# Running the joins between stages of a two-block transformer kernel in two halves of the tokens

## The chip, the cores and the metric

The kernel runs on one core of one Trainium2 chip. The metric is the device time of one execution in microseconds (us), over three runs. A profile is one further execution, recorded instruction by instruction. The engines are PE (matrix multiply; PEld is its weight load), DVE (elementwise), ACT (elementwise with functions), POOL (small elementwise work and some loads) and SP (which issues the weight loads).

## The reference, cut to what matters

256 tokens of width 1024, all in fp32. After a first block (mLSTM, attention and a mixture of experts) and a norm, two layers follow:

```
for l in range(2):
    x = x + 0.5 * rmsnorm(swiglu(rmsnorm(x, ffn1_pre_g[l]), w_ffn1_in[l], w_ffn1_out[l]), ffn1_post_g[l])
    h = rmsnorm(x, mix_pre_g[l])
    z, xbc, dt, rq, rk, rv, rg, aq, ak, av, gate = split(h @ w_in[l])
    ...                      # three mixers and their gated sum y
    x = x + rmsnorm(y @ w_out[l], mix_post_g[l])
    x = x + 0.5 * rmsnorm(swiglu(rmsnorm(x, ffn2_pre_g[l]), w_ffn2_in[l], w_ffn2_out[l]), ffn2_post_g[l])
```

Each `x = x + rmsnorm(...)` followed by the next `rmsnorm(x, ...)` is a join: the residual of a token needs that token's whole output row, and the next stage's first product needs the normalised row, transposed.

## The kernel before

A layer has three stages, called f1 (the first feed-forward), mx (the mixers) and f2. PE accumulates into 8 banks of 128 x 512 fp32. `LAYER_JOBS` lists all uses of the banks in order, and each engine waits on a bank's "full" or "read" counter. Weights come in units of 128 x 2048 (1 MB) through a ring of 6 slots; SP loads unit i into slot i % 6 once the unit 6 places before it is given back (`load_units`). A layer has 121 units, so its last unit sits in slot 0, the slot that the next layer's first unit wants; at the start of a layer SP waits for `ring_free`, raised by ACT at the end of f2.

Most products are done in three fp32r passes ("hi" and "lo" parts of both operands). `unit_hi` (ACT) rounds a unit to its hi part in one of 3 buffers, `unit_lo` (DVE) makes the lo part in `ring_r`. PE waits for the lo part (`unit_parts`). A feed-forward unit of the input projection takes 48 matmuls (2 halves of the bank, 8 slices of the depth, 3 passes) of 128x128 weights on 256 moving columns, the tokens (`split_columns`). The output projection keeps four banks, (n, t) for column half n and token half t, and goes through 11 units; each unit takes 24 matmuls on 512 moving columns, the tokens being the weights. mx begins with row products (rq first), also with tokens as weights and 512 moving columns: 12 matmuls for each unit and token half.

A join before the change runs in this order, all of it for the 256 tokens together:

- ACT squares the four output banks (`post_scalar`), DVE scales them into `xn` (`post_vector`), POOL makes the root (`post_pool`), DVE updates x for t = 0 and t = 1.
- ACT squares x for t = 0 and t = 1 (`row_squares`), after hi part 0 of the next stage, and then makes hi part 1; DVE has lo part 0 in its queue ahead of `scale_rows`; POOL makes the second root (`pre_pool`).
- DVE scales x into `xn`, t = 0 and 1; PE transposes 16 blocks into 4 banks (`turn_rows`); ACT writes the hi columns, DVE the lo columns, bank by bank; the first matmuls of the next stage wait for them bank by bank.

There are six such joins: from the experts into f1 of layer 0 (the chain there has one norm more, L2332, since the first block ends in its own norm), f1 to mx and mx to f2 in each layer, and f2 of layer 0 to f1 of layer 1, where the loop over the layers turns. After the last f2 only the update of x and the store of the output follow.

Of the kernel before, what the change touches and what calls it, by code (L numbers as in the profile page):

```python
# [8 lines left out]
P = 128  # L9
# [41 lines left out]
HI_BUFFERS = AHEAD_UNITS + 1  # L51

# [99 lines left out]

class Banks:
# [39 lines left out]
class Units:  # L193
# [4 lines left out]
    def __init__(self, landed_sems, parts_sem, units, base, parts_base, B, l=None):  # L198
        self.landed_sems, self.parts_sem, self.base, self.B, self.l = landed_sems, parts_sem, base, B, l
        self.parts_base = parts_base  # L200
# [3 lines left out]
        self.per = [len(range(s, len(units), SLOTS)) for s in range(SLOTS)]  # L204
        parts = [n for n in self.names if self.ends[n] is None]
        self.part = {n: i for i, n in enumerate(parts)}

    def slot(self, name):
        return self.index[name] % SLOTS

    def landed(self, name):

        i = self.index[name]
        n = self.base[i % SLOTS] + i // SLOTS + 1
        n = n if self.l is None else self.l * self.per[i % SLOTS] + n
        return self.landed_sems[self.slot(name)], n * 16

    def given_back(self, name):
# [4 lines left out]
        return self.parts_sem, (n if self.l is None else self.l * len(self.part) + n)  # L223

# [803 lines left out]
def moe_scalar(act, m, ps, M):  # L1028
    raise_ahead(act, M, "scalar")
    turns = act.value_load(m.r.turns_i[0:1, 1:2], min_val=PAIRS, max_val=PAIRS * PASSES)  # L1030
    with act.Fori(0, turns) as i:
# [24 lines left out]
def moe_tensor(pe, m, ps, M, landed):  # L1056
# [11 lines left out]
    with pe.Fori(0, turns) as i:  # L1068
# [13 lines left out]
        pe.wait_ge(M["added"], since(i * 4))  # L1082
# [73 lines left out]
def unit_hi(act, m, U, F, names, j, his):  # L1156

    if j >= HI_BUFFERS:
        act.wait_ge(*U.given_back(names[j - HI_BUFFERS]))
    act.wait_ge(*U.landed(names[j]))  # L1160
    act.activation(his[j % HI_BUFFERS], m.ring[U.slot(names[j])], ACT.Copy).then_inc(F["unit_hi"], 1)  # L1161


def unit_lo(dve, m, U, F, f, names, j, his):
# [3 lines left out]
    dve.tensor_tensor(m.ring_r[slot], m.ring[slot], his[j % HI_BUFFERS].bitcast(F32), ALU.subtract).then_inc(  # L1168
# [3 lines left out]
def unit_parts(pe, m, U, F, f, names, j, his, k):  # L1172

    pe.wait_ge(*F.at("unit_lo", SPLIT_BEFORE[f] + j + 1))
    return [v.rearrange("p (k n) -> p k n", k=k) for v in (his[j % HI_BUFFERS], m.ring_r[U.slot(names[j])])]


def split_columns(pe, B, ps, job, parts, moving, cols=None):


    hi, lo = parts
    for c in range(2):
        for k in range(KT):
# [12 lines left out]

def ffn_tensor(pe, m, ps, B, U, F, f):

    names = [f"{f}.n.{i}" for i in range(4)]
    units = ffn_unit_names(f)  # L1200
    turn_rows(pe, B, names, ps, m.xn, m.c["ident"], F, f)

    for i in range(FT):
# [3 lines left out]
        split_columns(pe, B, ps, job, parts, (m.hT_r, m.hTlo_r), [B.drained(n) for n in names] if i == 0 else None)  # L1207
    for i in range(FT // 2):
        hi, lo = unit_parts(pe, m, U, F, f, units, FT + i, m.whi_r, 2)
        for k in range(2):  # L1210
            kk = 2 * i + k
            pe.wait_ge(*F.at("ffn_hid", sofar(f, FT) + kk + 1))
            for n in range(2):
                for t in range(TT):
                    job = f"{f}.out.{n}.{t}"
                    if kk == 0:
                        B.claim(pe, job)
                    turns = passes_of([x[:, kk, t * P:(t + 1) * P] for x in (m.hid_r, m.hidlo_r)],
                                      [w[:, k, n * 512:(n + 1) * 512] for w in (hi, lo)])
                    for q, (x, w) in enumerate(turns):  # L1220
                        mm = pe.matmul(ps[B.bank(job)][:], x, w, start=kk + q == 0, stop=kk == FT - 1 and q == 2)  # L1221
                    if kk == FT - 1:
                        mm.then_inc(B.full(job), 1)
        if i < FT // 2 - 1:
            mm.then_inc(U.parts_sem, 1)


def ffn_scalar(act, step, m, ps, B, U, F, f, gain):
    units = ffn_unit_names(f)
    unit_hi(act, m, U, F, units, 0, m.whi_r)  # L1230
    row_squares(act, m, F, f)
    for j in range(1, AHEAD_UNITS):
        unit_hi(act, m, U, F, units, j, m.whi_r)
    for i in range(4):
        job = f"{f}.n.{i}"
        act.wait_ge(*B.filled(job))
        for k in range(2):
            ins = act.activation(m.hT_r[:, 2 * i + k, :], ps[B.bank(job)][:, k * T:(k + 1) * T], ACT.Copy,
                                 scale=gain[:, 2 * i + k:2 * i + k + 1])
        ins.then_inc(F[f"{f}.cols"], 1)  # L1240
# [13 lines left out]
    post_scalar(act, m, ps, B, F, f)  # L1254


def row_squares(act, m, F, f):

    for t in range(TT):
        act.wait_ge(*F.at(BEFORE[f] + ".x", t + 1 if f != "f1" else t - 1))  # L1260
        act.activation(m.hrows[:, t, :], m.x[:, t, :], ACT.Square, scale=D ** -0.5,
                       accum_out=m.ss[:, t:t + 1]).then_inc(F[f"{f}.ss"], 1)


def post_scalar(act, m, ps, B, F, f):

    for n in range(2):
        for t in range(TT):
            job = f"{f}.out.{n}.{t}"
            act.wait_ge(*B.filled(job))  # L1270
            act.activation(m.hrows[:, t, n * 512:(n + 1) * 512], ps[B.bank(job)][:], ACT.Square, scale=D ** -0.5,
                           accum_out=m.halves[:, n, t:t + 1]).then_inc(F[f"{f}.pss"], 1)
    if f == "f2":
        act.sem_inc(F["ring_free"], 1)


def ffn_vector(dve, step, m, ps, B, U, F, f, gain, post, post_landed=None):
    units = ffn_unit_names(f)
    unit_lo(dve, m, U, F, f, units, 0, m.whi_r)
    scale_rows(dve, m, F, f)  # L1280
    for i in range(4):
        job = f"{f}.n.{i}"
        dve.wait_ge(*F.at(f"{f}.cols", i + 1))
        for k in range(2):
            kk = 2 * i + k
            ins = dve.scalar_tensor_tensor(out=m.hTlo_r[:, kk, :], in0=ps[B.bank(job)][:, k * T:(k + 1) * T],  # L1286
# [1229 lines left out]
```

## Time and profile before

| what | value |
|---|---|
| median of three runs | 2398.27 us (2396.99 to 2401.87) |
| span of the profiled execution | 2400.0 us |
| busy: PE, DVE, ACT | 92%, 50%, 46% |
| POOL busy | 1% |
| mean DMA rate | 203 GB/s |

The profiled execution's own time is its span, 2400.0 us from first to last instruction, which is 1.7 us above the median and inside the range of the runs. A high busy share says that PE is the engine to look at, not that all of its time is needed.

### The profile page before, as it was taken

How to read it: one execution, taken by the hardware profiler on the slowest of the kernel's cores; microseconds unless marked ns; L12 is line 12 of the kernel's file. 1: busy time of each engine (PE TensorE's matmuls, PEld its weight loads, DVE VectorE, ACT ScalarE, POOL GpSimd, SP SyncE). 2: the span in 40 equal slices, each digit the busy share in tenths (PEclk: the TensorE clock that was granted, in tenths of full speed). 3: DMA queues.
4: the chain of work that ended last, by engine and by line, in shares of the span. 5: the costliest groups of instructions: out<-in, count | busy, mean ns of one | idle time of the engine just before them, and what ended most of it. 6: DMA issues, size and time to landing. Idle time of an engine off the chain costs nothing.

```text
span 2400.0 us, 33677 instructions
## 1 busy us (share of the span) xinstructions
PE 2212.8 (92%) x13178; PEld 1771.5 (74%) x13178; DVE 1198.0 (50%) x1568; ACT 1099.0 (46%) x1365; POOL 35.5 (1%) x59
## 2 busy tenths in 40 slices
PE   7857999999997998999999899979989999998998
PEld 6734444433445996898889799879968988897996
DVE  1152333333335664664745566456654655446663
ACT  1310000000004993454445599479734634364992
POOL 0000000000000000000000000000000000000000
PEclk9977999999999999999999999989989999998999
DMA  6205999999994554442235455355545422354552
GB/s 245 88 0 213 421 410 401 401 401 400 401 386 160 183 184 168 171 163 101 75 122 178 158 196 177 123 208 188 185 148 191 145 86 88 125 190 162 177 187 94
DMA packets 66920, 486.09 MB, mean 203 GB/s; under 512 B 7424, under 2 KB 7424, under 8 KB 8544
## 3 DMA queue, kind: packets, MB, share of 16 engines
q1 hardware_dynamic: 65632, 476.07, 52.8%
q0 software_dynamic: 1152, 8.16, 0.9%
q8 instruction: 91, 1.49, 0.2%
q14 instruction: 45, 0.37, 0.1%
HBM read 483.15 MB, written 1.05 MB: 202 GB/s over the span
## 4 chain that ended last, share of the span: by engine, by line
issue 68%; PE 26%; DVE 2%; ACT 2%; POOL 1%; DMA 0%; ACTq 0%; DVEq 0%; POOLq 0%; SPq 0%
PE bank L1077 9%; PE bank L1102 5%; PE bank L362 4%; PE bank L1051 3%; PE bank L1112 3%; PE bank L377 1%; PE bank L753 1%; PE bank L326 0%; ACT work L1042 0%; ACT work L1039 0%; DMA work<-in_first 0%; PE bank L1091 0%; ACT work L435 0%; POOL sums L308 0%; POOL sums L309 0%
## 5 line engine op out<-in xcount | busy, mean ns | idle before, releaser
L1188 PE MATMUL bank<-work_parts 128*128 128x256 f32 x2368 | 618.1, 283 | 0.0
L1168 DVE TENSOR_TENSOR ring_parts<-ring,work_parts 128x2048 fp32r<-128x2048 f32 x208 | 475.5, 2291 | 218.3 <-ACT work_parts L1161 197.6
L1161 ACT ACTIVATE work_parts<-ring 128x2048 fp32r<-128x2048 f32 x208 | 396.3, 1908 | 199.4 <-PE bank L1221 98.2
L1188 PEld LDWEIGHTS bank<-work_parts 128*128 128x128 f32 x2368 | 437.0, 192 | 0.1
L1188 PE MATMUL bank<-columns_parts,work_parts 128*128 128x256 f32 x1408 | 400.3, 284 | 2.3 <-DVE work_parts L1286 2.3
L1188 PE MATMUL bank<-columns_parts,ring_parts 128*128 128x256 f32 x1408 | 399.1, 283 | 0.0
L1188 PEld LDWEIGHTS bank<-columns_parts,work_parts 128*128 128x128 f32 x1408 | 271.0, 192 | 3.9 <-DVE work_parts L1286 3.8
L1188 PEld LDWEIGHTS bank<-columns_parts,ring_parts 128*128 128x128 f32 x1408 | 271.0, 192 | 0.0
L362 PE MATMUL bank<-columns,ring 128*128 128x256 f32 x1152 | 254.5, 383 | 1.2 <-ACT columns L344 1.2
L362 PEld LDWEIGHTS bank<-columns,ring 128*128 128x128 f32 x1152 | 220.7, 192 | 34.1 <-issue 3.7
L1221 PE MATMUL bank<-work_parts 128*128 128x512 f32 x704 | 217.4, 389 | 0.0
L1077 PE MATMUL bank<-ring,work 128*64 128x512 f32 x768 | 168.3, 594 | 1.1 <-DVE work L1024 1.1
L1221 PEld LDWEIGHTS bank<-work_parts 128*128 128x128 f32 x704 | 132.2, 188 | 27.4
L1077 PEld LDWEIGHTS bank<-ring,work 128*64 128x64 f32 x768 | 54.4, 137 | 112.5 <-issue 112.5
L1221 PE MATMUL bank<-ring_parts,work_parts 128*128 128x512 f32 x352 | 137.0, 389 | 0.0
L1019 DVE TENSOR_TENSOR x<-x,bank 128x512 f32<-128x512 f32 x64 | 44.0, 688 | 171.8 <-PE bank L1112 171.8
L1188 PE MATMUL bank<-rows_parts,work_parts 128*128 128x256 f32 x448 | 127.0, 283 | 0.0
L1188 PE MATMUL bank<-rows_parts,ring_parts 128*128 128x256 f32 x448 | 126.8, 283 | 0.0
L1102 PE MATMUL bank<-work 128*64 128x512 f32 x512 | 113.6, 594 | 14.1 <-ACT work L1039 14.1
L1382 PE MATMUL bank<-work_parts 128*128 128x512 f32 x320 | 115.7, 393 | 0.0
L1296 DVE TENSOR_TENSOR work<-work,bank 128x256 f32<-128x256 f32 x88 | 37.1, 422 | 155.2 <-ACT work L1251 155.2
L1250 ACT ACT_TABLE_LOAD x88 | 112.9, 1283 | 1.6
(355 smaller groups left out, 2917.9 us busy)
## 6 DMA issues: line engine op xcount, KB each, us to landing
ring<-in_w_layers SPq DMA_DIRECT2D x242, 1024.0 KB, 4.8
ring<-in_w_experts SPq DMA_DIRECT2D x96, 1024.0 KB, 8.0
work<-in_w_experts SPq DMA_DIRECT2D x96, 1024.0 KB, 9.1
ring<-in_w_first SPq DMA_DIRECT2D x16, 1024.0 KB, 4.9
work<-in_post POOLq DMA_DIRECT2D x3, 1024.0 KB, 5.0
work<-in_second POOLq DMA_DIRECT2D x1, 2944.0 KB, 14.3
work<-in_first SPq DMA_DIRECT2D x1, 1641.5 KB, 8.9
x<-in_x SPq DMA_DIRECT2D x1, 1024.0 KB, 5.0
```

Of the source, the lines that this page charges most:

```text
L362: mm = pe.matmul(ps[B.bank(job)][:, c * T:(c + 1) * T], w[:, k, c * P:(c + 1) * P], moving[:, k, :], start=k == 0, stop=k == KT - 1)
L1019: dve.tensor_tensor(xs, xs, ps[(SUM, TURN)[q % 2]][:], ALU.add).then_inc(M["added"], 1)
L1051: mm = pe.matmul(ps[GATHER + g][:, k * P:(k + 1) * P], m.xn[:, t, kk * P:(kk + 1) * P], m.sel[:, t, :], start=t == 0, stop=t == TT - 1)
L1077: mm = pe.matmul(ps[bank][e * 64:e * 64 + 64, :], m.hc[:, h * 4 + k, e * 64:e * 64 + 64], both[e][:, k, :], start=h + k == 0, stop=h * 4 + ...
L1102: mm = pe.matmul(ps[DOWN + n][e * 64:e * 64 + 64, :], m.hidT[:, ff * P + e * 64:ff * P + e * 64 + 64], both[e][:, f, n * 512:(n + 1) * 512 ...
L1112: pe.matmul(ps[(SUM, TURN)[q % 2]][:], m.selgT[:, t * P:(t + 1) * P], m.ym[:, n * 512:(n + 1) * 512], start=True, stop=True).then_inc(M["s ...
L1161: act.activation(his[j % HI_BUFFERS], m.ring[U.slot(names[j])], ACT.Copy).then_inc(F["unit_hi"], 1)
L1168: dve.tensor_tensor(m.ring_r[slot], m.ring[slot], his[j % HI_BUFFERS].bitcast(F32), ALU.subtract).then_inc(F["unit_lo"], 1)
L1188: mm = pe.matmul(ps[B.bank(job)][:, c * T:(c + 1) * T], w, x, start=k + n == 0, stop=k == KT - 1 and n == 2)
L1221: mm = pe.matmul(ps[B.bank(job)][:], x, w, start=kk + q == 0, stop=kk == FT - 1 and q == 2)
L1250: step(act.activation(e, e, ACT.Ln, bias=1.0))
L1382: mm = pe.matmul(ps[B.bank(jobs[t])][:], x, w, start=kk + n == 0, stop=kk == KT - 1 and n == 2)
```

## The change

At each join the tokens go in two halves of 128.

- The last products of a stage are reordered so that the banks of t = 0 are full first: in f1 and f2 the last two output units (`HELD_UNITS`) are held and used for t = 0, then t = 1 (12 matmuls a bank); in mx the last pair of units is used by half. A fourth hi buffer makes room for this.
- `bridge_scalar`, `bridge_vector` and `bridge_pool` replace the post and pre functions: roots of one column, x, its squares and `xn` for each half, t = 0 while PE still works on t = 1.
- In joins inside a layer hi and lo parts 0 and 1 of the next stage are made ahead of the bridge (`next_unit`), and the columns of half 0 inside it (`next_columns`). In f1, after the experts or the turn of the loop, they are made behind the bridge: two hi parts, then the columns.
- The next stage's first work goes by half: in f1 and f2 units 0 and 1 are multiplied on 128 tokens at a time (`split_half`, same weights loaded again for the other half); in mx, rq goes by half, still on 512 moving columns.
- `LAYER_SLOTS` puts two neighbouring units into slot 0, so that the next layer's first units find slots given back earlier. `ring_free` goes.

```diff
-def split_columns(pe, B, ps, job, parts, moving, cols=None):
...
+def split_half(pe, B, ps, job, parts, moving, t, ready=None):
+    bank = ps[B.bank(job)]
+    tokens = slice(t * P, (t + 1) * P)
     for c in range(2):
         for k in range(KT):
+            if ready and c == 0 and k % 2 == 0:
+                pe.wait_ge(*ready[k // 2])
+            for n, (w, x) in enumerate(passes_of([w[:, k, c * P:(c + 1) * P] for w in parts],
+                                                 [x[:, k, tokens] for x in moving])):
+                mm = pe.matmul(bank[:, c * T + t * P:c * T + (t + 1) * P], w, x, ...)
...
 def ffn_tensor(pe, m, ps, B, U, F, f):
-    turn_rows(pe, B, names, ps, m.xn, m.c["ident"], F, f)
-    for i in range(FT):
+    turn_half(pe, B, ps, m, F, f, 0)
+    split_half(pe, B, ps, f"{f}.in.0", parts0, moving, 0, [F.at("half_lo", ...) for i in range(4)])
+    turn_half(pe, B, ps, m, F, f, 1)
+    split_half(pe, B, ps, f"{f}.in.1", parts1, moving, 0)
+    split_half(pe, B, ps, f"{f}.in.0", parts0, moving, 1, [B.drained(f"{f}.n.{i}") for i in range(4)])
+    split_half(pe, B, ps, f"{f}.in.1", parts1, moving, 1)
+    for i in range(2, FT):
...
+    held = [unit_parts(pe, m, U, F, f, units, FT + i, m.whi_r, 2) for i in range(held_from, FT // 2)]
+    for t in range(TT):
+        for n in range(2):
+            for i in range(held_from, FT // 2):
+                for kk in (2 * i, 2 * i + 1):
+                    mm = out_matmuls(held[i - held_from], kk, n, t)
...
+            mm.then_inc(B.full(f"{f}.out.{n}.{t}"), 1)
 def ffn_scalar(...):
+    if f == "f1":
+        for j in range(AHEAD_UNITS):
+            unit_hi(act, m, U, F, units, j, m.whi_r)
+        ffn_columns_scalar(act, m, ps, B, F, f, gain, 0)
+    ffn_columns_scalar(act, m, ps, B, F, f, gain, 1)
...
+def bridge_scalar(act, m, ps, B, F, f, next_columns):
+    for n, t in OUT_ORDER[f]:
+        act.wait_ge(*B.filled(job))
+        act.activation(m.xn[:, t, n * 512:(n + 1) * 512], ps[B.bank(job)][:], ACT.Square, ...)
+        if n == 1:
+            if t == TT - 1 and next_columns:
+                next_columns(0)
+            act.wait_ge(*F.at(f"{f}.x", t + 1))
+            act.activation(m.xn[:, t, :], m.x[:, t, :], ACT.Square, ...).then_inc(F[f"{f}.ss"], 1)
...
+def bridge_vector(dve, m, ps, B, F, f, post, weight, next_columns):
+    def scaled(t):
+        dve.wait_ge(*F.at(f"{f}.rstd", t + 1))
+        dve.tensor_scalar(m.xn[:, t, :], m.x[:, t, :], m.ss[:, t:t + 1], None, ALU.mult).then_inc(F[f"{f}.xn"], 1)
+    for n, t in OUT_ORDER[f]:
+        if (n, t) == (1, 1):
+            scaled(0)
+        dve.wait_ge(*squared(F, f, n, t))
+        dve.scalar_tensor_tensor(out=m.xn[:, t, c], in0=ps[B.bank(job)][:], ...)
+        if n == 1:
+            dve.wait_ge(*F.at(f"{f}.prstd", t + 1))
+            dve.scalar_tensor_tensor(out=m.x[:, t, :], in0=m.xn[:, t, :], ...).then_inc(F[f"{f}.x"], 1)
+    if next_columns:
+        next_columns(0)
+    scaled(1)
+def bridge_pool(pool, step, m, F, f):
+    for t in range(TT):
+        pool.wait_ge(*squared(F, f, 0, t))
+        step(pool.tensor_tensor(m.pr[:, t:t + 1], m.halves[:, 0, t:t + 1], m.c["eps"][:, 0:1], ALU.add))
+        pool.wait_ge(*squared(F, f, 1, t))
+        step(pool.tensor_tensor(m.pr[:, t:t + 1], m.pr[:, t:t + 1], m.halves[:, 1, t:t + 1], ALU.add))
+        pool.tensor_tensor(m.pr[:, t:t + 1], m.pr[:, t:t + 1], m.half[:, 0:1], ALU.pow).then_inc(F[f"{f}.prstd"], 1)
+        pool.wait_ge(*F.at(f"{f}.ss", t + 1))
+        root_of_mean_of(pool, step, m, m.ss, t, F[f"{f}.rstd"])
...
+TWICE = 15
+LAYER_SLOTS = [i % SLOTS if i < TWICE else 0 if i == TWICE else (i - 1) % SLOTS for i in range(len(LAYER_UNITS))]
```

## Rows read from the trace of the kernel before

**Rows 1.** PE's waits: engine, line, whom it waited for; total us, times, longest

```profile
PE bank L326 <- DVE rows L1312: 60.1, 6, 14.0
```

**Rows 2.** Windows at four joins: us, busy by engine, PEclk, DMA share, GB/s

```profile
946.00:954.80 8.80, 0.00 (x0) 0.00 (x1) 7.09 (x8) 6.62 (x9) 2.98 (x5) 0.73 0.34 119
1364.20:1373.00 8.80, 0.00 (x0) 0.01 (x1) 6.35 (x6) 6.58 (x8) 2.99 (x5) 0.63 0.34 120
1564.20:1578.20 14.00, 0.06 (x1) 0.00 (x0) 6.97 (x8) 6.57 (x10) 2.59 (x6) 0.63 0.92 349
2202.40:2206.00 3.60, 3.49 (x16) 3.49 (x17) 3.60 (x8) 3.13 (x5) 0.54 (x1) 0.50 0.02 5
```

**Rows 3.** Timeline, join f1 to mx, layer 0: start, us, instruction, [idle before]

```profile
946.03 0.60 ACT L1271 ACTIVATE columns<-bank 128x512 f32<-128x512 f32 x1
...
946.80 0.19 POOL L1343 TENSOR_TENSOR post_roots<-half_sums 128x2 f32<-128x2 f32 x1 [192.92 <-ACT columns L1271]
...
948.18 2.48 DVE L1329 SCALAR_TENSOR_TENSOR x<-rows,post_roots,x 128x1024 f32<-128x1024 f32 x2 [0.73 <-POOL post_roots L309]
...
950.69 1.06 ACT L1261 ACTIVATE columns<-x 128x1024 f32<-128x1024 f32 x1
950.78 2.29 DVE L1168 TENSOR_TENSOR ring_parts<-ring,work_parts 128x2048 fp32r<-128x2048 f32 x1
...
951.92 1.21 POOL L308 TENSOR_TENSOR sums<-sums,const 128x2 f32<-128x2 f32 x1 [3.88 <-ACT columns L1261]
...
953.93 1.42 DVE L1312 TENSOR_SCALAR rows<-x,sums 128x1024 f32<-128x1024 f32 x2 [0.86 <-POOL sums L309]
...
954.83 3.65 PE L326 MATMUL bank<-const,rows 128*128 128x128 f32 x16 [8.83 <-DVE rows L1312]
```

**Rows 4.** Timeline: PE's last matmuls (one left out between) and the store

```profile
2390.12 0.39 PE L1221 MATMUL bank<-work_parts 128*128 128x512 f32 x1
...
2390.58 0.39 PE L1221 MATMUL bank<-work_parts 128*128 128x512 f32 x1
...
2395.57 0.41 SPq L2268 DMA_DIRECT2D out<-x  x1
```

**Rows 5.** Timeline, ACT: the hi part that waits until rq is finished

```profile
972.82 1.92 ACT L1161 ACTIVATE work_parts<-ring 128x2048 fp32r<-128x2048 f32 x1 [3.52 <-PE bank L1382]
```

**Rows 6.** Timeline, ACT: input units 0 and 1 read from their banks

```profile
765.21 0.39 ACT L1249 ACTIVATE work<-bank 128x256 f32<-128x256 f32 x1 [3.23 <-PE bank L1188]
...
1383.47 0.39 ACT L1249 ACTIVATE work<-bank 128x256 f32<-128x256 f32 x1 [3.23 <-PE bank L1188]
...
1389.23 0.38 ACT L1249 ACTIVATE work<-bank 128x256 f32<-128x256 f32 x1
...
1588.71 0.39 ACT L1249 ACTIVATE work<-bank 128x256 f32<-128x256 f32 x1 [3.21 <-PE bank L1188]
```

**Rows 7.** Timeline: last add of the experts; hi part 0 of layer 1

```profile
744.03 0.69 DVE L1019 TENSOR_TENSOR x<-x,bank 128x512 f32<-128x512 f32 x1 [0.17 <-PE bank L1112]
...
1569.90 1.91 ACT L1161 ACTIVATE work_parts<-ring 128x2048 fp32r<-128x2048 f32 x1 [4.91 <-DMA ring<-in_w_layers]
```

**Rows 8.** Timeline, PE: streams of 1 and of 128 moving fp32 columns

```profile
153.07 2.74 PE L796 MATMUL bank<-const,work 128*128 128x1 f32 x24
...
1146.24 1.95 PE L1492 MATMUL bank<-ring,columns 128*128 128x128 f32 x16
```

**Rows 9.** Lines by form, PEld: weight loads, count, busy us, mean ns, idle before

```profile
L1188 PEld LDWEIGHTS bank<-work_parts 128*128 128x128 f32 x2368 | 437.0, 192 | 0.1
...
L796 PEld LDWEIGHTS bank<-const,work 128*128 128x128 f32 x24 | 2.8, 192 | 0.0
...
L1561 PEld LDWEIGHTS bank<-const,work 128*128 128x128 f32 x64 | 7.0, 140 | 1.6 <-issue 1.6
```

**Rows 10.** Timeline, join mx to f2: hi and lo columns

```profile
1375.42 3.02 ACT L1238 ACTIVATE columns_parts<-bank,work 128x256 fp32r<-128x256 f32 x8 [3.60 <-PE bank L326]
1376.29 3.23 DVE L1286 SCALAR_TENSOR_TENSOR work_parts<-bank,work,columns_parts 128x256 fp32r<-128x256 f32 x8 [2.76 <-ACT columns_parts L1238]
```

More of the change, by code:

```diff
@@ L203, in __init__ @@
         self.index = {n: i for i, n in enumerate(self.names)}
-        self.per = [len(range(s, len(units), SLOTS)) for s in range(SLOTS)]
+        self.per = [slots.count(s) for s in range(SLOTS)]
         parts = [n for n in self.names if self.ends[n] is None]
@@ L1206, in ffn_tensor, with out_matmuls @@
         parts = unit_parts(pe, m, U, F, f, units, i, m.whi_r, KT)
[L1207 to L1211, printed above, removed]
+        split_columns(pe, B, ps, job, parts, moving)
+    def out_matmuls(parts, kk, n, t):
+        job = f"{f}.out.{n}.{t}"
+        turns = passes_of([x[:, kk, t * P:(t + 1) * P] for x in (m.hid_r, m.hidlo_r)],
+                          [w[:, kk % 2, n * 512:(n + 1) * 512] for w in parts])
+        for q, (x, w) in enumerate(turns):
+            mm = pe.matmul(ps[B.bank(job)][:], x, w, start=kk + q == 0, stop=kk == FT - 1 and q == 2)
+        return mm
+    for n in range(2):
+        for t in range(TT):
+            B.claim(pe, f"{f}.out.{n}.{t}")
+    held_from = FT // 2 - HELD_UNITS
+    for i in range(held_from):
+        parts = unit_parts(pe, m, U, F, f, units, FT + i, m.whi_r, 2)
+        for kk in (2 * i, 2 * i + 1):
             pe.wait_ge(*F.at("ffn_hid", sofar(f, FT) + kk + 1))
@@ L1214, in ffn_tensor, with ffn_scalar @@
                 for t in range(TT):
[L1215 to L1228, printed above, removed]
-    units = ffn_unit_names(f)
[L1230 to L1240, printed above, removed]
+                    mm = out_matmuls(parts, kk, n, t)
+        mm.then_inc(U.parts_sem, 1)
+    held = [unit_parts(pe, m, U, F, f, units, FT + i, m.whi_r, 2) for i in range(held_from, FT // 2)]
+    pe.wait_ge(*F.at("ffn_hid", sofar(f, FT) + FT))
+    for t in range(TT):
+        for n in range(2):
+            for i in range(held_from, FT // 2):
+                for kk in (2 * i, 2 * i + 1):
+                    mm = out_matmuls(held[i - held_from], kk, n, t)
+                if (t, n) == (1, 1) and i < FT // 2 - 1:
+                    mm.then_inc(U.parts_sem, 1)
+            mm.then_inc(B.full(f"{f}.out.{n}.{t}"), 1)
+def ffn_scalar(act, step, m, ps, B, U, F, f, gain, next_unit, next_columns):
+    units = ffn_unit_names(f)
+    if f == "f1":
[3 more added lines that the diff above has]
+    ffn_columns_scalar(act, m, ps, B, F, f, gain, 1)
     for i in range(FT):
@@ L1253, in ffn_scalar @@
         unit_hi(act, m, U, F, units, j, m.whi_r)
[L1254 to L1274, printed above, removed]
@@ L1291, in ffn_vector @@
+def ffn_vector(dve, step, m, ps, B, U, F, f, gain, post, next_unit, next_columns, post_landed=None):
+    units = ffn_unit_names(f)
+    if f == "f1":
+        for j in range(AHEAD_UNITS):
+            unit_lo(dve, m, U, F, f, units, j, m.whi_r)
+        ffn_columns_vector(dve, m, ps, B, F, f, gain, 0)
+    ffn_columns_vector(dve, m, ps, B, F, f, gain, 1)
     for i in range(FT):
```

423 lines of the change are left out of this document (264 added, 159 removed).

## The prediction

> **What bounds the kernel now.** I read PE's waits first, since PE is busy longest (the table above). The largest single wait is that of the transposes for the normalised rows: six times, 60.1 us in all, up to 14.0 [rows 1]. [...] The timeline of one join shows why: a chain of small operations with one owner at a time. From the last matmul (at 946.0) it is the square 0.8 us, POOL 1.4, x 2.5 for both halves, two squares 2.5, POOL 2.0, the first `xn` 0.9, and then 3.65 us of transposes at half clock [rows 3]. Outside the joins PE waits little, so a join is worth what it delays PE's next full stream, and extra PE work in it counts in full once that stream is reached. After the last matmul (2391.0) 4.6 us pass before the store is issued [rows 4].
>
> So I measure a join by one number: U, the time from the end of the last matmul of the old stage until the next stage's first two units are multiplied (rq, or input units 0 and 1). Before:
>
> - f1 to mx: 972.8 - 946.0 = 26.8 [rows 5].
> - mx to f2: unit 0 is read at 1383.5, unit 1 5.76 later [rows 6], the old stage ended at 1364.2 [rows 2]: 25.0. In layer 1 the clock is still at 0.50 in 3.6 us of these matmuls [rows 2], which costs 1.8: 26.8. f1 to mx in layer 1 I take as in layer 0.
> - experts to f1: the last add starts on PE's last product, 744.0; 765.2 + 5.8 - 744.0 = 27.0. Turn of the loop: 1588.7 + 5.8 - 1564.2 = 30.3, and there hi part 0 was held up by its load, to 1569.9 [rows 7].
>
> Sum of the six: 162.7 us.
>
> **The change part by part.** *The price of a matmul on 128 columns.* `split_half` turns the 96 matmuls of two units (0.120 each: 5.76 / 48 [rows 6]) into 192 on 128 columns, with each weight block loaded twice. No fp32r matmul of fewer than 256 columns is in the trace. [...] An fp32 stream on 128 columns goes at (1.95 - 0.27) / 15 = 0.112 [rows 8]. [...] From above, fp32 does in two such instructions what fp32r does in one: 0.224. I take 0.112, the nearest row. So the halves cost 192 x 0.112 = 21.5 us against 11.5, 10.0 more in each of four joins, and this is what the earlier start has to pay.
>
> [...]
>
> *mx to f2.* Times count from the old stage's last matmul. Banks of 12 matmuls at 0.23 [rows 4] end at -5.5 (t = 0 complete) and 0. For t = 0: square and POOL to x in 1.9 (one add less than the 2.15 from 946.03 to 948.18), x 1.24, square 1.23 (950.69 to 951.92), POOL 1.1 (1.38 from 946.80 to 948.18, one add less): `xn` starts at +0.1, PE's transposes at +1.0 [rows 3]. ACT then has 8 half columns at 0.25 (0.377 for whole ones, less half of the 256 elements' part), DVE 8 at 0.27 [rows 10]. DVE comes to them only when x of t = 1 is done: 1.9 + 1.24 = 3.1. First lo columns, and first matmuls, at 3.75, the last at 5.35. ACT's square of x for t = 1 stands behind its columns (3.5), POOL follows, DVE's `xn` stands behind its lo columns: transposes of t = 1 at 6.75, which PE reaches at 8.7, so it does not wait for them. After the eight transposes ACT and DVE have 5 us, under input unit 1 of t = 0, for the columns of t = 1 (4 us). PE: 5.35 + 0.7 + 24 x 0.112 + 0.9 (8 transposes) + 144 x 0.112 = 25.8. PE idles 1 us and then nearly 2: the clock may fall again. In [rows 2] it fell in every stand of 8.8 us or more, and 3.6 us of matmuls at the low level cost 1.8. No row shows a stand of 1 to 2 us between full streams, so the charge lies between 0 and twice that; I take 1.4. U = 27.2, against 25.0 and 26.8: +2.2 and +0.4.
>
> *f1 to mx.* Hi and lo 0 and 1 are ready ahead: their hi buffers come free 72 and 48 matmuls before the end (16.4 and 10.9 us), their ring slots earlier still; a load that ACT had to wait out took 4.9 us [rows 7], so SP is in time. `xn` of t = 0 stands behind one more scaling on DVE: transposes at 1.25. DVE makes two operations of 256 elements per bank here (0.40 each [rows 10]): first lo columns 4.1, then 0.8 apart; `xn` of t = 1 stands behind them. rq loses nothing in halves, since the 512 moving columns are weights: 12 x 0.228 from 4.1, transposes of t = 1 at 7.4, 36 x 0.228 after them: 16.5, plus 1.3 for the clock: 17.8. Against 26.8 that is -9.0, twice. The units behind it are not late: DVE's columns of t = 1 end at about 12, its lo part 2 (2.3) at 14.6, before rq ends.
>
> *Experts to f1.* Here the bridge makes no parts. ACT's queue holds the square for t = 0 and 1, the square of x for t = 0 and 1, then hi 0 and 1 (1.9 each [rows 7]), then the columns. Before, both hi parts stood inside the waits for POOL. From 744.0: last add 0.7, square and POOL 2.8, x 1.25, square 1.2: ACT is free at 6.1, hi parts end at 10.0, lo part 1 (2.29 [rows 3]) at 12.8, lo columns 13.4 to 15.0. PE: 15.0 + 0.7 + 2.7 + 0.9 + 16.1 = 35.4, and after 9 us without a stream the clock is low at the start, as in [rows 2]: I take 5.4 us at the low level, +2.7, between 1.8 and 3.6. U = 38.1 against 27.0: +11.1.
>
> *Turn of the loop.* The same with x of t = 1 at 3.1: ACT free at 4.5, hi parts to 8.4, lo to 11.1, lo columns to 13.3, U = 33.7 + 2.7 = 36.4 against 30.3: +6.1. Parts and columns were mixed with the chain before; now nothing of them runs under it. The change of the slots takes the load's delay off the path (unit 0 can be loaded some 27 us before the end), but the parts now queue behind the squares.
>
> *Tail.* x of t = 1 is done at 1.9 + 1.24 = 3.1 instead of 4.6: -1.4. The extra squares and scaling run beside the store.
>
> *POOL* has 19 chained steps for 10 in a layer. One add took 1.21 us instead of 0.19 while DVE worked on two SBUF operands [rows 3]; in the new order such pairs meet at most twice in a join off the critical step, and I take 0 with 0 to 4 us in all. [...]
>
> Sum: 2 x -9.0 + 2.2 + 0.4 + 11.1 + 6.1 - 1.4 = +0.4 us on 2400.0. On the median of 2398.3 that is 2398.7.
>
> **The rivals.** [...]
>
> *Dear halves.* fp32r on 128 columns at the pace of fp32, 0.224: +0.112 x 768 = +86, 2485, slower from 0.119 up. Against: nothing in the trace, for there is no such matmul; for it: nothing either.
>
> *The late start in f1 decides.* If the clock stays low longer after these joins (in layer 1 it was still low when matmuls had run for 3.6 us behind the transposes [rows 2]), or the price is 0.12 like a 256 column matmul, or POOL blocks: +6 to +14, 2408. For it: the two joins where parts queue behind the squares have no slack at all.
>
> [...]
>
> **How the numbers follow.** A measurement of this kernel tells 0.2% (4.8 us) from no change. Forecast (within 4.8 us) 0.30; cheap halves 0.22; clock holds 0.12; late start 0.26; dear halves 0.10. Faster 0.34, same 0.30, slower 0.36. The range takes in all but dear halves and the far end of cheap ones: 2372 to 2416; the forecast's own is 2394 to 2403.
>
> **What would show it.** [...] U of each join: 17.8 at f1 to mx (a chain of waits over 22 would say that the bridge is not hidden), 27 at mx to f2, 36 to 38 into f1. ACT's hi parts 0 and 1 after the squares in f1, with PE standing 9 us. The store issued 3.1 us after the last matmul. If U into f1 is under 32 at 0.112, my queue order is wrong; if a stream after a join shows new waits, the gain is given back there.

## The result, and the profile after

The changed kernel takes 2444.1 us (median of 4 runs, 2433.6 to 2466.1), the kernel before 2399.9 beside it (4 runs, 2397.0 to 2401.9): a ratio of 1.019, 95% interval 1.014 to 1.024. It is slower by 44 us; forecast was no change, and 2444 lies outside the range given (2372 to 2416). The profiled execution has a span of 2440.7 and an own time of 2442.4.

PE's waits after, the lines that take the place of [rows 1]:

```profile
PE bank L1235 <- DVE work_parts L1428: 20.8, 4, 12.2
...
PE bank L1262 <- DVE rows L2524: 5.9, 1, 5.9
...
PE bank L1262 <- DVE rows L1439: 3.6, 5, 0.9
```

The waits did what they should: the transposes wait 9.5 us in all instead of 60.1, and the half units 20.8 (two long ones of them into f1). PE stands some 30 us less and the kernel is 44 us longer. So the time must be in PE's own work. The windows, which stand beside [rows 2]: first the join from the experts to f1, then mx to f2 of layer 0, last of layer 1.

```profile
754.70:765.00 10.30, 10.27 (x48) 10.27 (x49) 1.52 (x6) 0.00 (x0) 0.00 (x0) 0.50 0.01 2
765.00:767.70 2.70, 2.70 (x16) 2.70 (x15) 1.32 (x6) 1.98 (x8) 0.00 (x0) 0.52 0.00 0
767.70:778.00 10.30, 10.30 (x95) 10.30 (x94) 3.13 (x5) 1.99 (x2) 0.00 (x0) 1.00 0.01 2
...
1380.00:1400.60 20.60, 20.60 (x99) 20.60 (x98) 4.13 (x9) 2.98 (x6) 1.15 (x2) 0.50 0.17 58
1400.60:1410.80 10.20, 10.20 (x50) 10.20 (x50) 3.85 (x5) 5.58 (x6) 0.00 (x0) 0.50 0.30 104
1410.80:1412.80 2.00, 2.00 (x11) 2.00 (x11) 0.00 (x0) 1.86 (x3) 0.00 (x0) 0.52 0.29 57
1412.80:1417.00 4.20, 4.20 (x37) 4.20 (x36) 1.98 (x5) 3.73 (x4) 0.00 (x0) 1.00 0.54 224
...
2218.30:2259.30 41.00, 41.00 (x195) 41.00 (x195) 8.49 (x15) 11.47 (x18) 1.15 (x2) 0.50 0.18 58
```

What matters here is PE's count against the granted clock (PEclk is the third column from the end). At 0.50 the halves go at 10.3 / 48 = 0.214 us each. At full clock they go at 0.112, as forecast, by their starts: every third matmul of the first f1 join is in the row below, and 45 steps of three in 15.1 us are 0.112. (A window also counts the matmuls that reach over its edges, so 10.3 / 95 would be too low.)

```profile
L1235 PE MATMUL bank<-columns_parts,ring_parts x46: 272/276/280, 768.0 to 783.1; 128*128 128x128 f32 x46
```

At both mx to f2 joins the clock stays at 0.50 for 41 us, in which PE does not stand at all. It did not fall in the stand: PE stood 0.7 us before the first transposes and 1.9 us behind them, and the first 18 half matmuls still ran at full clock. It fell 1.9 us into the half stream:

```profile
1369.80:1371.70 1.90, 1.88 (x17) 1.90 (x18) 1.72 (x7) 0.67 (x2) 0.73 (x2) 1.00 0.28 116
1371.80:1410.80 39.00, 39.00 (x185) 39.00 (x185) 8.66 (x15) 9.55 (x15) 1.15 (x2) 0.50 0.17 58
```

It came back 2 us after the stream of whole units had begun (1410.8). In the two joins into f1 it came back earlier, in the middle of the halves: behind the first 48, the eight transposes and five or six more (at 767.6 in the first). The forecast had low levels of 2.8 and 5.4 us in these joins.

The joins by the timeline, mostly ACT's rows, which answer to [rows 5, 6]; each pair begins with the square that reads the last product of the old stage (the turn of the loop has three):

```profile
958.49 0.60 ACT L1383 ACTIVATE rows<-bank 128x512 f32<-128x512 f32 x1 [0.77 <-PE bank L1303]
...
976.29 1.92 ACT L1193 ACTIVATE work_parts<-ring 128x2048 fp32r<-128x2048 f32 x1 [1.16 <-PE bank L1505]
...
1366.09 0.60 ACT L1383 ACTIVATE rows<-bank 128x512 f32<-128x512 f32 x1 [1.03 <-PE bank L1505]
...
1410.91 0.38 ACT L1346 ACTIVATE work<-bank 128x256 f32<-128x256 f32 x1 [4.60 <-PE bank L1235]
...
1586.88 0.60 ACT L1383 ACTIVATE rows<-bank 128x512 f32<-128x512 f32 x1 [0.70 <-PE bank L1303]
...
1593.93 3.71 ACT L1193 ACTIVATE work_parts<-ring 128x2048 fp32r<-128x2048 f32 x2 [2.97 <-issue]
...
1629.93 0.36 ACT L1346 ACTIVATE work<-bank 128x256 f32<-128x256 f32 x1
...
2432.94 0.39 PE L1303 MATMUL bank<-work_parts 128*128 128x512 f32 x1
...
2436.29 0.41 SPq L2443 DMA_DIRECT2D out<-x  x1
```

U by join, read in this way from each kernel's trace (experts to f1 from the last add, 742.35 after); "whole" and "early" are experiments below:

| join | before | forecast | after | whole | early |
|---|---|---|---|---|---|
| experts to f1 | 26.9 | 38.1 | 41.2 | 27.9 | 25.1 |
| f1 to mx, layer 0 | 26.8 | 17.8 | 17.8 | 19.1 | 16.6 |
| mx to f2, layer 0 | 25.0 | 27.2 | 44.8 | 21.9 | 22.0 |
| turn of the loop | 30.2 | 36.4 | 43.1 | 29.9 | 27.0 |
| f1 to mx, layer 1 | 26.4 | 17.8 | 17.9 | 19.2 | 16.6 |
| mx to f2, layer 1 | 26.4 | 27.2 | 44.8 | 20.4 | 21.8 |
| sum | 161.7 | 164.5 | 209.6 | 138.4 | 129.1 |

The store is issued 3.0 us after the end of PE's last matmul (2433.3), before 4.6 [rows 4]. The prediction had 162.7 for the sum before: its two joins of layer 1 were estimates, and both are 26.4 in the trace. The sum of the joins rises by 47.9, less 1.6 of the tail is 46.3. The spans of the two profiles differ by 40.7, so nothing was lost outside the joins; after is some 6 us shorter there, mostly in mx (1.6 and 3.7 us), where its clock was low for a shorter time.

### The profile page after: what moved, and what is told of

The parts are those of the page before. It is cut to its first block, busy times and chain, and to the rows that moved or that the text cites. A ratio compares the mean times of both kernels' runs of the same rounds, so it can differ in the third digit from the quotient of the medians.

```text
span 2440.7 us, 34674 instructions
## 1 busy us (share of the span) xinstructions
PE 2285.2 (94%) x13562; PEld 1846.3 (76%) x13562; DVE 1205.4 (49%) x1618; ACT 1107.0 (45%) x1417; POOL 43.1 (2%) x95
## 4 chain that ended last, share of the span: by engine, by line
PE 75%; issue 19%; DVE 3%; ACT 2%; POOL 1%; DMA 0%; ACTq 0%; DVEq 0%; POOLq 0%; SPq 0%
PE bank L1220 20%; PE bank L388 13%; PE bank L1109 9%; PE bank L1505 7%; PE bank L1134 5%; PE bank L1303 4%; PE bank L1235 3%; PE bank L1083 3%; PE bank L1144 3%; PE bank L403 1%; PE bank L874 1%; PE bank L780 0%; PE bank L1723 0%; PE bank L1684 0%; PE bank L1605 0%
## 5 line engine op out<-in xcount | busy, mean ns | idle before, releaser
L1220 PE MATMUL bank<-work_parts 128*128 128x256 f32 x2240 | 581.9, 283 | 0.0
L1220 PEld LDWEIGHTS bank<-work_parts 128*128 128x128 f32 x2240 | 412.5, 192 | 0.1
L1220 PE MATMUL bank<-columns_parts,work_parts 128*128 128x256 f32 x1280 | 363.4, 284 | 0.0
L1220 PE MATMUL bank<-columns_parts,ring_parts 128*128 128x256 f32 x1280 | 363.0, 284 | 0.0
L1220 PEld LDWEIGHTS bank<-columns_parts,work_parts 128*128 128x128 f32 x1280 | 246.8, 193 | 0.0
L1220 PEld LDWEIGHTS bank<-columns_parts,ring_parts 128*128 128x128 f32 x1280 | 246.5, 193 | 0.0
L1303 PEld LDWEIGHTS bank<-work_parts 128*128 128x128 f32 x704 | 132.2, 188 | 27.3
```

The lines of the kernel that those rows point to most:

```text
L1220: mm = pe.matmul(out, w, x, start=k + n == 0, stop=k == KT - 1 and n == 2)
```

## The experiments

Two theories stood for the lost 45 us. One: the clock is low and a stream of matmuls on 128 columns does not lift it, so the price is 0.214 for 0.112 (the clock). The texts below say "a stream that starts at the low clock"; as shown above, at mx to f2 it starts at the full clock and is soon at the low one. The other: that form is dear in itself, or the waits into f1 are the loss.

**whole.** The changed kernel, but both halves are transposed first and input units 0 and 1 are multiplied whole. In f1 the second half's transposes wait for the lo columns of the first, since both write into the same banks.

```
     turn_half(pe, B, ps, m, F, f, 0)
+    turn_half(pe, B, ps, m, F, f, 1)
...
+        elif f == "f1":                      # in turn_half, t = 1
+            pe.wait_ge(*F.at("half_lo", ...))
...
-    split_half(pe, B, ps, f"{f}.in.0", parts0, moving, 0, [... half_lo ...])
-    turn_half(pe, B, ps, m, F, f, 1)
-    B.claim(pe, f"{f}.in.1")
-    parts1 = ...
-    split_half(pe, B, ps, f"{f}.in.1", parts1, moving, 0)
-    split_half(pe, B, ps, f"{f}.in.0", parts0, moving, 1, [...])
-    split_half(pe, B, ps, f"{f}.in.1", parts1, moving, 1)
-    for i in range(2, FT):
+    split_columns(pe, B, ps, f"{f}.in.0", parts0, moving, [B.drained(f"{f}.n.{i}") for i in range(4)])
+    for i in range(1, FT):
```

> The change with only the heads of f1 and f2 put back to whole units: input units 0 and 1 on 256 columns, after both halves are transposed; bridge, mx and slots stay. Clock theory (a stream of matmuls on 128 columns that starts at the low clock never lifts it, 0.213 us each, while at the full clock it costs 0.112): U at mx to f2 falls from 45 us to 21 to 22, into f1 from 41 to 43 down to 30, the clock is back within 6 us of the first matmul; total 2375, faster than the kernel before. Rival (the longer queues of the bridge cost the time, whatever the columns): U into f1 stays near 40 and the total at 2410 or more.

Measured: 2373.3 us (2372.3 to 2374.9), ratio to before 0.989, interval 0.987 to 0.991. Two windows of its join mx to f2, layer 0:

```profile
1361.40:1368.20 6.80, 6.54 (x30) 6.14 (x31) 4.17 (x10) 3.97 (x9) 1.15 (x2) 0.51 0.18 41
1368.20:1372.00 3.80, 3.80 (x35) 3.80 (x33) 0.40 (x1) 0.38 (x1) 0.00 (x0) 1.00 0.60 244
```

The clock falls here too, but comes back after 6.8 us, under a stream on 256 columns. Taking the half units out of the change brings 71 us and makes it faster than the kernel before. U at mx to f2 fell to 21.9 and 20.4 and into f1 to 27.9 and 29.9, with the queues of the bridge unchanged, so the rival falls. The loss is in the half units; what is left of the change gains.

**halves_first.** The kernel before with input units 0 and 1 by halves, nothing else of the change:

```
-        split_columns(pe, B, ps, job, parts, (m.hT_r, m.hTlo_r), [...])
+        if i in (0, 1):
+            for t in range(TT):
+                split_half(pe, B, ps, job, parts, (m.hT_r, m.hTlo_r), t, [...])
+        else:
+            split_columns(pe, B, ps, job, parts, (m.hT_r, m.hTlo_r), [...])
```

> The kernel before with input units 0 and 1 of f1 and f2 multiplied on 128 columns, t = 0 then t = 1, and nothing else changed. Clock theory: where the clock is back when the first unit starts the join costs 10 us more (192 x 0.112 for 96 x 0.12), where it is not 28 to 30 more, as the stream holds it down; 1 or 2 of the 4 joins low: total 2440 to 2500, likeliest 2458, and runs that differ among themselves. Rival (plain work, 0.112 everywhere): 2440 in every run, clock as before. Second rival (0.213 whatever the clock): 2518.

Measured: 2498.0 (2497.0 to 2499.0), ratio 1.040, interval 1.039 to 1.042. Three of the four joins went low, not one or two, and the runs agree among themselves: U is 37.0 from the experts (26.9 in the kernel before), where the clock stayed up, and 52.2, 59.7 and 52.2 in the others (25.0, 30.2, 26.4).

**halves_mid.** The same edit with `i in (10, 11, 12, 13)`: twice as many half units, in the middle of a stream.

> The kernel before with input units 10 to 13 of each f1 and f2 on 128 columns in two halves, 16 units in all, each starting at the full clock in the middle of a stream. If the price at full clock is 0.112 and the stream keeps the clock: 16 x (10.75 - 5.76) = +80, 2480. If a stream on 128 columns also lets a full clock fall: up to 16 x (20.5 - 5.76) = +236, 2636.

Measured: 2476.6 (2 runs, 2474.0 and 2479.3), ratio 1.032, interval 1.029 to 1.034. A window of the half matmuls of halves_mid, then two lines of its source view (count; least, median and longest ns, first and last start), of the whole span and of its first group alone, and windows of halves_first: its first join, then transposes, first halves and two long stretches of later joins:

```profile
820.00:830.00 10.00, 10.00 (x92) 10.00 (x91) 3.85 (x5) 4.94 (x6) 0.00 (x0) 1.00 0.26 82
```

```profile
L1204 PE MATMUL bank<-work_parts x512: 273/275/280, 817.1 to 2362.2; 128*128 128x128 f32 x171
L1204 PE MATMUL bank<-columns_parts,ring_parts x128: 273/274/277, 817.3 to 859.8; 128*128 128x128 f32 x128
```

```profile
759.40:770.00 10.60, 10.60 (x92) 10.48 (x93) 6.66 (x8) 2.99 (x5) 0.00 (x0) 1.00 0.00 0
...
1383.00:1387.50 4.50, 3.65 (x16) 3.28 (x16) 1.74 (x4) 1.48 (x5) 0.00 (x0) 0.51 0.00 0
1387.50:1390.90 3.40, 3.07 (x24) 2.96 (x25) 3.40 (x8) 3.35 (x6) 0.12 (x1) 0.99 0.00 0
1390.90:1431.90 41.00, 41.00 (x194) 41.00 (x194) 8.39 (x10) 10.38 (x12) 1.03 (x2) 0.50 0.24 81
...
1609.40:1667.40 58.00, 48.38 (x226) 47.98 (x227) 15.19 (x18) 19.58 (x26) 3.41 (x3) 0.50 0.33 127
```

These two settle the form. In mid stream 1536 half matmuls run (three groups of 512, the longest 280 ns, so all at full clock), at 0.112 (127 steps of three in 42.5 us), and cost 76 us for 16 units: 4.7 a unit (96 x 0.112 - 5.76 is 5.0). At the joins 768 of them cost 97 us for 8 units, 12.2 a unit. The instruction is the same; what differs is where the stream stands. In the first join the stream met a full clock and kept it. In the second the clock had risen (1387.5) and fell again after 24 half matmuls paced by their lo columns, and then the 168 left, without a gap, did not lift it. Why the first kept it and the second did not stays open. The kernel before shows the same join with whole units: there, too, the clock was back behind the transposes, and it stayed:

```profile
1373.00:1376.70 3.70, 3.65 (x16) 3.26 (x16) 0.94 (x3) 1.28 (x4) 0.00 (x0) 0.50 0.00 0
1376.90:1389.00 12.10, 11.78 (x96) 11.74 (x97) 8.57 (x13) 8.82 (x12) 1.15 (x2) 1.00 0.50 186
```

**warm.** The changed kernel with 2 (f2) or 5 (f1) matmuls on constants, 512 columns wide, ahead of the first half unit, where PE stands anyway; their result is overwritten.

```
     B.claim(pe, f"{f}.in.0")
+    for i in range(5 if f == "f1" else 2):
+        pe.matmul(ps[B.bank(f"{f}.in.0")][:], m.const[:, 0:P], m.const[:, 0:512], start=True, stop=True)
```

> The change with extra matmuls on constants (512 columns, results overwritten) in the stand between the first transposes and the first half unit: 2 in f2 (1.9 us, the length of the stand), 5 in f1 (4.6 us). The halves stay. Clock theory: both joins mx to f2 keep the full clock and their U falls from 45 to 27; f1 of layer 0 gains about 6, f1 of layer 1, whose stand is 12 us long, little; total about 2400, clock low for 41 us nowhere. Rival (128 columns cost 0.213 for themselves): U stays at 45 and the total rises by up to 5 from 2444.

Measured: 2410.8 over ten runs, ratio 1.005, interval 1.002 to 1.007; five runs lie at 2400.8 to 2403.6 and five at 2417.9 to 2421.3. The profiled one is of the lower five. A third of its half matmuls (source view), and the same group after (lines by form: busy us, mean ns):

```profile
L1235 PE MATMUL bank<-work_parts x256: 272/275/420, 757.5 to 2219.1; 128*128 128x128 f32 x128
```

```profile
L1235 PE MATMUL bank<-work_parts 128*128 128x128 f32 x256 | 91.6, 358 | 0.0
```

The median is 275 ns (a whole duration, which overlaps the next; the pace is 0.112), where after has a mean of 358. At both mx to f2 joins the clock stayed up for all 192 halves and U is 26.4, for 44.8 in after and 27 expected; into f1 U is 36.4, and 43.4 at the turn of the loop, where, as expected, the fill was too short: PE stood 8.5 us more behind it, and the granted clock was at 0.50 from 1577.8 on. A few wide matmuls, which only add work, take 33 us off in the median and 41 in the lower five. So the loss to the low clock is shown by an edit that leaves every half matmul in place. The upper five runs differ from the lower by the clock too: (1 - mean granted clock) x span is 76.9 us in them and 60.0 in the lower five, an estimate from the runs' own clocks (0.968 and 0.975), and between the groups lie 16.5 us. That is the size of one join at the low level, but which one it was is not known, as no profile of such a run was taken.

**one_half.** The changed kernel with unit 0 by halves and unit 1 whole.

```
-    B.claim(pe, f"{f}.in.1")
-    parts1 = ...
-    split_half(pe, B, ps, f"{f}.in.1", parts1, moving, 0)
     split_half(pe, B, ps, f"{f}.in.0", parts0, moving, 1, [...])
-    split_half(pe, B, ps, f"{f}.in.1", parts1, moving, 1)
-    for i in range(2, FT):
+    for i in range(1, FT):
```

> The changed kernel with input unit 0 alone by halves (in both f1 and f2) and unit 1 whole, so half as many matmuls on 128 columns. Theory (a stream on 128 columns that starts at the low clock goes at 0.213 each and stays there until wide matmuls lift the clock): mx to f2 starts at 5.4, 48 matmuls of 10.2, transposes 1.8, 48 of 10.2, unit 1 7: U about 35, 13 to 15 over 'whole' in each layer; into f1 the second 48 are at full speed as in the changed kernel, U about 39 and 41, 11 more in each: 2420 in all, 2410 to 2430. Rival (the clock falls only where all 192 matmuls stand together; half of them keep it up): U of 23.5 at mx to f2, 2395 to 2400. Second rival (the price of halves at full clock alone, and the low stretch is the wait's and not the narrow stream's): four joins with 5.0 us more each than 'whole', less what the earlier start gives: 2385 to 2395.

Measured: 2427.5 (2420.0 to 2431.3), ratio 1.011, interval 1.007 to 1.014. Windows at mx to f2 of layer 0, then into f1:

```profile
1386.00:1403.20 17.20, 17.12 (x80) 16.72 (x80) 5.05 (x11) 8.43 (x15) 1.15 (x2) 0.50 0.36 131
1403.30:1410.00 6.70, 6.70 (x58) 6.70 (x58) 3.16 (x4) 4.42 (x6) 0.00 (x0) 1.00 0.32 104
758.99:769.20 10.21, 10.21 (x48) 10.21 (x48) 1.50 (x6) 0.00 (x0) 0.00 (x0) 0.50 0.01 2
769.30:785.40 16.10, 16.02 (x75) 15.62 (x75) 4.46 (x9) 7.49 (x14) 0.00 (x0) 0.50 0.14 48
```

U is 34.4 and 32.8 at mx to f2, 42.7 and 44.4 into f1. Both rivals fall: half as many halves do not hold the clock, and the low stretches end 3 to 5 us into unit 1, whole. Into f1 the clock did not rise behind the second transposes, as it had after (767.6); the theory had that wrong, by 3.7 and 3.4 us of U (39 and 41 expected), which is the 7 us over the likeliest value.

**early.** "whole" with a shorter chain into f1: ACT makes hi part 0, the square of x for t = 1, the columns, and hi part 1 last; DVE likewise.

```
-        for j in range(AHEAD_UNITS):
-            unit_hi(act, m, U, F, units, j, m.whi_r)
+        unit_hi(act, m, U, F, units, 0, m.whi_r)
+        row_squares_of(act, m, F, "f2", 1, F.at("f2.x", 0))
         ffn_columns_scalar(act, m, ps, B, F, f, gain, 0)
     ffn_columns_scalar(act, m, ps, B, F, f, gain, 1)
+    if f == "f1":
+        unit_hi(act, m, U, F, units, 1, m.whi_r)
...                                           # the same for DVE and POOL, and in the bridge
```

> The changed kernel with input units 0 and 1 multiplied whole, as in the run 'whole' (2373.3), and with a shorter chain into f1 on ScalarE and VectorE: in f1 ScalarE makes hi part 0, then the square of x for the second half of the tokens, then the columns of both halves, and hi part 1 last; VectorE makes lo part 0, the second half's scaled rows, the columns, and lo part 1 last. Nothing is left out. Theory (the serial order of parts behind the squares is what holds U into f1 at 27.9 and 29.9 in 'whole'): one hi part (1.9 us) and one lo part (2.3 us) go from before the stream to beneath it, U into f1 drops by 3 to 4 us from the experts and by 4 to 8 us at the turn of the loop, each once: about 2361, between 2356 and 2366. Rival (the transposes and the clock hold the stream up, the parts don't): the time stays within 2 us of 'whole', 2371 to 2375. Second rival: unit 1's lo part is now late under unit 0's 5.8 us of matmuls and makes a wait of its own, giving 1 to 3 us back at each join into f1: 2365 to 2369.

Measured: 2364.5 (2362.2 to 2364.9), ratio 0.984, interval 0.982 to 0.987. PE's waits of whole, then of early:

```profile
PE bank L1266 <- DVE work_parts L1427: 16.8, 2, 12.3
```

```profile
PE bank L1266 <- DVE work_parts L1443: 12.1, 2, 9.9
```

The two waits into f1 fall by 4.7 us, U into f1 by 2.8 and 2.9. The theory holds in kind and is too large: of the 4 to 8 at the turn of the loop only 2.9 came. The two joins f1 to mx, whose code is that of whole, fall by another 5 us in sum: there the clock fell in whole and not in early (windows of layer 0, whole and then early). The new order of the parts is not shown to be the cause of this:

```profile
948.40:955.20 6.80, 6.14 (x17) 4.91 (x18) 3.42 (x9) 1.40 (x4) 0.73 (x2) 0.51 0.39 148
```

```profile
950.80:957.00 6.20, 6.16 (x30) 4.99 (x31) 4.81 (x13) 3.18 (x11) 0.75 (x2) 1.00 0.31 127
```

**The slots, and the clock in early.** `whole_old_slots` and `early_old_slots` have the ring slots of the kernel before:

```
-LAYER_SLOTS = [i % SLOTS if i < TWICE else 0 if i == TWICE else (i - 1) % SLOTS for i in ...]
+LAYER_SLOTS = [i % SLOTS for i in range(len(LAYER_UNITS))]
```

> 'whole' with the ring slots of the kernel before. Theory: in 'whole' hi part 0 stands behind ScalarE's two squares of x at the turn of the loop and its load is there by then with either slots: 0 to 1 us over 'whole', 2373 to 2374.5. Rival: the load is late as before and the slots are worth 3 to 6 us: 2376 to 2379.

> 'early' with the ring slots of the kernel before, so that the weights of f1's unit 0 can be loaded only later at the turn of the loop. Theory: with parts no longer queued behind both squares, the late load is seen again at the turn of the loop, where hi part 0 was held up until 1569.9 in the kernel before: 2 to 5 us over 'early', once. Rival (SP's overhead at the loop's turn sets the load in either order of slots): within 1 us of 'early'.

Measured: 2372.9 (ratio 0.988) and 2365.3 (0.985): within 1 us of whole and early. But the totals hide a loss that the traces show. With the old slots ACT waits for loads at the join from the experts, where neither theory looked for it (hi part 0, whole_old_slots and then early_old_slots; in whole and early no such wait is there):

```profile
748.82 1.91 ACT L1193 ACTIVATE work_parts<-ring 128x2048 fp32r<-128x2048 f32 x1 [1.45 <-DMA ring<-in_w_layers]
```

```profile
748.88 1.91 ACT L1193 ACTIVATE work_parts<-ring 128x2048 fp32r<-128x2048 f32 x1 [3.46 <-DMA ring<-in_w_layers]
```

U there is 29.1 for 27.9 and 28.4 for 25.1; at the turn of the loop it is 32.3 for 29.9 and 27.3 for 27.0. So by U the new slots are worth some 3.5 us in both pairs, one profile each, of which the turn of the loop has 2.4 and 0.3. In the totals other things stood against it: in the profile of whole_old_slots the clock stayed up at f1 to mx of layer 0 (U 16.5 for 19.1) and fell in layer 1, and in that of early the first block, which the edit does not touch, ended 4.8 us later than in early_old_slots (last add at 746.7 for 741.9). `early_fill` puts wide matmuls on constants into the stands of early, `early_again` is early beside it:

```
+    if f == "f1":
+        B.claim(pe, f"{f}.n.0")
+        fill(f"{f}.n.0", 5)
     turn_half(pe, B, ps, m, F, f, 0)
     B.claim(pe, f"{f}.in.0")
+    fill(f"{f}.in.0", 2 if f == "f1" else 4)
     turn_half(pe, B, ps, m, F, f, 1)
```

> 'early' (2364.5) with matmuls on constants where TensorE stands in a join, their results overwritten: into f1 five before the transposes of the first half (the stand was 5.9) and two between the two halves' transposes (2.15), into f2 four between the halves' transposes (4.33). Nothing else differs. Theory (each stand lets the clock fall, and the transposes and the first matmuls behind it run at the low level): the two f1 joins lose 10.2 and 13.7 us of low clock, the mx to f2 joins 6.8 each; transposes of 1.97 and 2.24 become 1.1, and the first dozen wide matmuls go at 0.12 for 0.213: 2 to 3 us off each of four joins, 2354, between 2351 and 2358. Rival (the clock falls in the stand all the same, or the fill ends later than the operand it waits for and delays the transposes): 2363 to 2369.

> 'early' once more, beside 'early_fill', so that the two can be compared on the same chip: 2364.5 by every theory, between 2362 and 2367; whether the clock falls at f1 to mx (it did not in the first profile of 'early', it did in 'whole') is open, and a profile that shows 6.8 us of low clock there would say that it is chance.

Measured: 2360.2 (2358.7 to 2362.6) and 2361.0 (2359.9 to 2362.1), ratios 0.984 both. Into f1, PE's rows of early_fill:

```profile
750.00 1.09 PE L1266 MATMUL bank<-const,rows 128*128 128x128 f32 x8 [1.56 <-DVE rows L2549]
750.93 1.88 PE L1286 MATMUL bank<-const 128*128 128x512 f32 x4
754.19 2.20 PE L1266 MATMUL bank<-const,rows 128*128 128x128 f32 x8 [1.38 <-DVE work_parts L1449]
756.26 0.58 PE L1222 MATMUL bank<-columns_parts,work_parts 128*128 128x256 f32 x1
```

The first transposes are now at full clock (1.09 for 1.97 in early). The second ones take 2.20 because they wait in pairs for the lo columns; the clock is still up under them, and falls behind them:

```profile
754.20:755.70 1.50, 1.30 (x6) 0.59 (x6) 1.50 (x7) 1.03 (x4) 0.00 (x0) 1.00 0.00 0
755.90:759.20 3.30, 3.30 (x16) 3.04 (x16) 2.16 (x9) 3.19 (x6) 0.00 (x0) 0.50 0.02 5
```

So the first matmuls of the stream are at half clock as in early, and U into f1 is 25.2 and 26.5 for 25.1 and 27.0. At mx to f2 the clock held, and unit 0 was read 13.3 us after the first transposes instead of 15.3. Of these two joins of 2 us, 1.4 is lost again at f1 to mx of layer 1, where the clock fell in this profile (U 18.0 for 16.6); the difference of medians is 0.8, with spreads of 4 and 2, and the fill is not shown to be worth anything. With the stream wide, the low clock cost a join 1.4 to 2.6 us here, by these numbers: at f1 to mx U was 18.0 in early_fill and 19.1 and 19.2 in whole, where the clock fell, for 16.6 where it stayed up, and at mx to f2 unit 0 was read 2.0 later in early.

early_again is 3.5 us under early. Its joins are those of early to 0.1 us; its first block was 4.9 us shorter in the profile (last add at 741.75 for 746.70). At f1 to mx the clock stayed up in both layers in early, early_again and early_old_slots; in whole it fell in both, in whole_old_slots in layer 1 alone. The best versions that ran are early and early_fill, 36 to 40 us under the kernel before.

## Why the prediction was wrong

**The step that failed** is the charge for the clock: "I take 1.4" at mx to f2, "between 0 and twice that", and "+2.7, between 1.8 and 3.6" into f1. Its bounds came from [rows 2], where 3.6 us of matmuls ran at the low level. In the kernel before, the clock was back at the end of the 16 transposes or up to 3.6 us into a stream on 256 columns, and that stream kept it. I carried the duration of the low level over to a stream on 128 columns, for which there was no row. What it measured: at mx to f2, 174 matmuls at 0.214 for 0.112 are 17.7 us, and the eight transposes between them took 1.9 for 1.0: 18.6 us against the 1.4 taken; U came out 17.6 over the forecast, twice. Into f1, the first 48 matmuls, eight transposes and five or six matmuls more ran low: 6.3 us for a charge of 2.7; U came out 3.1 and 6.7 over. These four make 45.0 us; the clock accounts for 2 x 17.2 and 2 x 3.6 of them, 41.6, and most of the rest is the later start at the turn of the loop (below).

**The price of a half matmul** was right: 0.112 taken from the fp32 row on 128 columns, 0.112 measured at full clock. Cheap halves, a lower price, to which 0.22 was given, did not occur. The dear halves rival named 0.224, two fp32 instructions (the 16 of the second line of [rows 8] are 8 products), and 2485; 0.214 did occur, but at a granted clock of 0.50 and not by the form: in halves_mid the same form goes at 0.112, all of it at 1.00.

**f1 to mx** was right to 0.1 us, 17.8 and 17.9, with the bridge hidden as said, and not by luck: where the clock stayed up (early) U is 16.6, against 16.5 without the 1.3 charged for it. **The tail** was right: 3.0 for 3.1. **The order of the queues into f1** was right: two hi parts behind the squares and PE standing 12.2 us at most. The first half matmul began 12.4 after the last add, about a microsecond ahead of my working. **At the turn of the loop** ACT began its hi parts 7.05 after the last square (1593.93), where I had 4.5: 2.97 of it is idle time at the head of the new layer for which the profile has no releaser. I had nothing for it in the sum; this is the second, smaller error, 2.5 us. In whole ACT idles 3.1 and in early 4.2 at the same place, so 1.1 of early's missing gain went there. What this time is made of was not tried. **The slots** were right in kind: with the new ones ACT waits for no load at either join into f1.

**POOL** I took at nothing, 0 to 4 us. Of the 16 adds that stand for the one of 1.21 in [rows 3], two took 0.39 and 0.79 and the others 0.18 to 0.24: under 1 us in all.

**The rivals.** "The late start in f1 decides" had the right mechanism in its first condition, a clock that stays low longer, but at 2408 it put the price where [rows 2] ended. "The clock holds" did not occur: the granted clock was 0.50 for 41 us in both mx to f2 joins. With the clock up at both mx to f2 joins (the lower runs of warm) the change is at 2402.7, within 0.2% of the forecast of 2398.7. So the forecast was that of a kernel whose clock comes back; that the two agree so well is in part luck, since U at the turn of the loop is still 43.4 for 36.4 there and the parts outside the joins are shorter than I had them.

## What to carry to other kernels

Splitting the first units of a stage so that they can start earlier is only worth it if the smaller matmuls are cheap enough: here 128 for 256 columns cost 4.7 us a unit at full clock, and 12.2 on average where PE came from a stand. Take the gain from the chain by halves (squares, norm, transposes) and leave the matmuls whole: that turned +44 us into -27, and with the parts' order mended into -36 to -39, of which 5 are a clock that stayed up at f1 to mx (U 16.6 for 19.1 and 19.2) and not shown to be the order's. Read two versions' joins one by one before calling a part worth nothing: the slots' 3.5 us did not show in the totals. Before a form of matmul that the trace doesn't have is put behind a wait, price it at both levels of the clock (here 0.112 and 0.214), the whole stream long, and keep the low one in the range.

## What the runs showed of the hardware

The granted clock did not go by PE's busy share: PE was busy without a gap at 0.50 (1371.8 to 1410.8 after) and at 1.00 (817.1 to 859.8 in halves_mid). With matmuls on 128 columns it stayed at 0.50 for 41 us in both mx to f2 joins after (1371.8 to 1412.8 and 2218.3 to 2259.3), and as long in halves_first (1390.9 to 1431.9), the first matmuls on 256 columns behind them included. In these joins it had been at 1.00 for the stream's first 18 or 24 matmuls; at the turn of the loop in halves_first it was at 0.50 from the first matmul on (1622.7) and stayed so for all 192. It came back 2 to 5 us after matmuls on 256 columns had begun: 2.1 and 2.2 after, 3.7 to 5.0 in halves_first, 3 to 5 in one_half. The same 128 column stream, entered at 1.00 out of a dense stream, kept that level for all of its 43 us (halves_mid, 817.1 to 859.8), and so it did at mx to f2 behind 1.9 us of matmuls on 512 columns (warm, 1.00 from 1369.9 to 1391.5). In the two f1 joins after, the clock came back behind the transposes between the halves (at 767.6 and 1614.1), and in one_half and at mx to f2 it did not (0.50 from 769.3 to 781.6 and from 1380.0 to 1400.6); why, stays open, as does whether it falls in the short stands at f1 to mx (it did for 6.8 us in both layers in whole, in neither in early, and in one of the two in whole_old_slots, with the same code there).
